# Constant multiplications on TensorE at the waits of a two-block transformer kernel on one Trainium2 core

## The reference

```python
def reference(x, ...):
    for layer in range(2):                     # first block
        h = rms_norm(x, norm1_g)
        mq, mk, mv, mo, mi, mf, aq, ak, av = split(h @ w_in)
        y_m = gated, normed mLSTM of silu(conv(mq, mk)), mv, mo, both directions
        y_a = dilated_attention(rope(aq), rope(ak), av)          # 8 heads of 64
        x = x + concat(y_m, y_a) @ w_out
        u = relu(rms_norm(x, norm2_g) @ w_up)                    # 1024 -> 4096
        x = x + (u * u) @ w_down
    x = rms_norm(x, final_g)
    x = layer_norm(ALPHA * x + pool_mixer(x))  # second block, layer 0
    x = layer_norm(ALPHA * x + swiglu(x))                        # hidden 2816
    x = layer_norm(ALPHA * x + nsa_mixer(x))   # layer 1: 16 heads, compressed,
                                               # selected and window attention
    return layer_norm(ALPHA * x + moe_ffn(x))  # 8 experts of 3584, top 2
```

## Time and profile before

| | us |
|---|---|
| median of three runs | 2382.86 (2381.65 to 2383.4) |
| profiled execution, its own time | 2385.09 |
| span of its instructions | 2383.0 |
| TensorE busy (matmuls) | 2145.7 |
| VectorE busy | 1599.2 |
| ScalarE busy | 1322.9 |

### The profile page before, as it was taken

The page is one execution under the profiler, slowest core; times in us unless marked ns, Lnnn a source line. Parts: engine busy times, 40 slices in busy tenths (PEclk is TensorE's granted clock), DMA queues, the critical chain, the costliest instruction groups (busy, mean ns, idle before and its releaser), DMA issues.

```text
span 2383.0 us, 25823 instructions
## 1 busy us (share of the span) xinstructions
PE 2145.7 (90%) x9918; PEld 1731.7 (73%) x9918; DVE 1599.2 (67%) x1539; ACT 1322.9 (56%) x1374; POOL 22.1 (1%) x33
## 2 busy tenths in 40 slices
PE   6888999988999799897868999999999888888986
PEld 5667887766888688776657887787888676766665
DVE  3865545765555545565645554887888788888987
ACT  4554444544444344445524444676776677777876
POOL 0000000000000000000000000000000000000000
PEclk9989999988999899996988999999999999999999
DMA  6314553422654345341007655798888789898995
GB/s 236 147 45 146 177 194 125 177 80 77 235 192 177 115 179 192 142 160 40 1 18 270 206 211 180 289 366 316 350 344 346 302 347 385 329 385 329 410 368 218
DMA packets 74356, 524.53 MB, mean 220 GB/s; under 512 B 8704, under 2 KB 9152, under 8 KB 11872
## 3 DMA queue, kind: packets, MB, share of 16 engines
q1 hardware_dynamic: 71424, 511.64, 56.7%
q0 software_dynamic: 2784, 10.93, 1.3%
HBM read 521.48 MB, written 1.05 MB: 219 GB/s over the span
## 4 chain that ended last, share of the span: by engine, by line
PE 71%; DVE 15%; ACT 8%; issue 5%; DMA 0%; DVEq 0%; ACTq 0%
PE psum L517 51%; PE psum L527 9%; DVE LO L507 6%; ACT HI L499 4%; PE psum L1008 2%; DVE AR L1479 1%; PE psum L2284 1%; PE psum L1013 1%; PE psum L799 1%; PE psum L2312 1%; PE psum L862 1%; DVE XT L690 1%; ACT AR L828 1%; PE psum L675 1%; PE psum L1841 1%
## 5 line engine op out<-in xcount | busy, mean ns | idle before, releaser
L507 DVE TENSOR_TENSOR LO<-ring,HI 128x2048 fp32r<-128x2048 f32 x379 | 851.7, 2258 | 453.2 <-ACT HI L499 451.1
L499 ACT ACTIVATE HI<-ring 128x2048 fp32r<-128x2048 f32 x379 | 712.7, 1886 | 369.0 <-PE psum L517 278.8
L517 PE MATMUL psum<-HI,XT 128*128 128x512 f32 (+1 forms) x2592 | 841.6, 400 | 64.6 <-DVE XT L690 30.2
L517 PEld LDWEIGHTS psum<-HI,XT 128*128 128x128 f32 x2592 | 502.5, 195 | 182.6 <-DVE XT L690 34.2
L517 PE MATMUL psum<-LO,XT 128*128 128x512 f32 (+1 forms) x1296 | 513.4, 396 | 0.0
L517 PEld LDWEIGHTS psum<-LO,XT 128*128 128x128 f32 x1296 | 253.2, 195 | 50.2
L527 PE MATMUL psum<-HI,XT 128*128 128x512 f32 x560 | 237.9, 425 | 56.5 <-DVE LO L507 55.7
L507 DVE TENSOR_TENSOR LO<-AR,HI 128x2048 fp32r<-128x2048 f32 x112 | 254.3, 2289 | 49.9 <-ACT HI L499 49.4
L499 ACT ACTIVATE HI<-AR 128x2048 fp32r<-128x2048 f32 x112 | 213.2, 1911 | 62.0 <-PE psum L527 38.0
L527 PE MATMUL psum<-LO,XT 128*128 128x512 f32 x560 | 227.9, 407 | 0.0
L517 PE MATMUL psum<-HI,HTH 128*128 128x512 f32 x568 | 225.1, 396 | 0.0
(11 more groups left out here) (271 smaller groups left out, 1829.7 us busy)
## 6 DMA issues: line engine op xcount, KB each, us to landing
ring<-in_experts SPq DMA_DIRECT2D x224, 1024.0 KB, 6.1
ring<-in_dense SPq DMA_DIRECT2D x149, 1024.0 KB, 4.8
AR<-in_experts SPq DMA_DIRECT2D x112, 1024.0 KB, 6.1
bcs<-in_ln_g POOLq DMA_DIRECT2D x4, 512.0 KB, 4.4
bcs<-in_ln_b POOLq DMA_DIRECT2D x4, 512.0 KB, 5.0
bcs<-in_norm_g POOLq DMA_DIRECT2D x3, 512.0 KB, 3.8
cons<-in_cons POOLq DMA_DIRECT2D x1, 1317.0 KB, 8.1
X<-in_x SPq DMA_DIRECT2D x2, 512.0 KB, 4.3
```

What stands on the lines that cost most here:

```text
L499: e.activation(HI[:, h:h + m], slot(u), ACT.Copy).then_inc(*high.up(u))
L507: e.tensor_tensor(LO[:, h:h + m], slot(u), HI[:, h:h + m].bitcast(F32), ALU.subtract).then_inc(*low.up(u))
L517: ins = e.matmul(out_ap, lhsT=a, rhs=b, start=start and n == 0, stop=stop and n == m - 1)
```

## The change

TensorE gets additional fp32 multiplications of constants by constants (`ident` by the first 512 columns of `cons`), written to a PSUM bank that nothing reads. `idle(e, n)` issues n of them; `idle_first(e, n)`, used while only the identity has landed, issues n of 128x128. The bank is the next of the rotation, through `Banks.hold`, without moving the rotation on; the bank is then marked "idle", and the next to hold it doesn't wait. `turn_rows` gets `wait` (multiplications before its transposes, none unless given) and `rest` (after them, one unless given).

```diff
     def hold(self, e, b, *use):
         before = self.use.get(b)
-        if before is not None:
+        if before is not None and before[0] != "idle":
             for s in self.emptied:
                 e.wait_ge(*s.of(*before))
+    def next(self, e, *use):
+        return self.hold(e, self.n % 4, *use)
...
+        def idle(e, n):
+            if n:
+                bank = banks.next(e, "idle")
+                e.wait_ge(s_cons, 16)
+                for _ in range(n):
+                    e.matmul(bank, lhsT=ident, rhs=cons[:, 0:512], start=True, stop=True)
+        def idle_first(e, n):
+            bank = banks.next(e, "idle")
+            e.wait_ge(s_ident, 16)
+            for _ in range(n):
+                e.matmul(bank[:, 0:P], lhsT=ident, rhs=ident, start=True, stop=True)
-        def turn_rows(e, name, t, src, ready):
+        def turn_rows(e, name, t, src, ready, wait=0, rest=1):
+            idle(e, wait)
...
                 ins.then_inc(*filled.up(name, "cols", t, k0))
+            idle(e, rest)
```

The places, in TensorE's order:

```diff
 # first block, layer l
+            if l == 0:
+                idle_first(e, 10)
-            turn_rows(e, n1, 0, lambda k: ROWS[:, 0, tile(k)], rows_at(n1, 0))
+            turn_rows(e, n1, 0, lambda k: ROWS[:, 0, tile(k)], rows_at(n1, 0), rest=l)
+            if l == 0:
+                idle_first(e, 18)
+            def second_rows():
+                turn_rows(e, n1, 1, lambda k: ROWS[:, 1, tile(k)], rows_at(n1, 1), wait=l, rest=l)
+                if l == 0:
+                    idle_first(e, 4)
...
             cols(e, ("aq", l), ...)
+            idle(e, 1)
             scores_tensor(e, l)
             cols(e, ("ak", l), ...)
             spread_sums_tensor(e, l, 1)
+            idle(e, 1)
             cols(e, ("av", l), ...)
...
+            def gather_last():
+                idle(e, 1)
+                ml_gather_tensor(e, l, 3)
+            steps = {1: lambda: ml_turn_tensor(e, l, 3), 2: gather_last, 7: lambda: idle(e, 1),
+                     9: lambda: idle(e, 1)}
...
 # y.l: rest=1 after tile 0, rest=0 after tile 1
 # n2.l: tile 0 rest=1; tile 1 wait=1, rest=1
 # pooling
+            idle(e, 5)                         # at the start of pool_tensor
 # l0: tile 0 wait=2, rest=3; tile 1 rest=1
 # l1: tile 0 rest=1; tile 1 wait=2, rest=1
+            idle(e, 1)                         # after cols kvc, before the turns of the queries
+                idle(e, 1 if kind or gp else 2)  # in blocks_tensor, before each of four banks
+            idle(e, 4 if qt else 2)            # at the start of turn_c_tensor
 # y.2: rest=3 after tile 0, rest=1 after tile 1
 # l2: tile 0 rest=1; tile 1 wait=6, rest=1
+            idle(e, 2)                         # at the start of route_tensor
+            idle(e, 3)                         # after route_tensor, before the first fetches
+            idle(e, 4)                         # after the fetches, before the first expert
```

More of the change, by code:

```diff
@@ L1291, in rows_at @@
                 return [v_done.of(name, "rows", t)]
-            turn_rows(e, n1, 0, lambda k: ROWS[:, 0, tile(k)], rows_at(n1, 0))
-            cols_by_tile(e, ("raw", l, 0), ("qk", l, 0), BOTH, xr, between=lambda: turn_rows(
-                e, n1, 1, lambda k: ROWS[:, 1, tile(k)], rows_at(n1, 1)))
+            if l == 0:
[7 more added lines that the diff above has]
+                    idle_first(e, 4)
+            cols_by_tile(e, ("raw", l, 0), ("qk", l, 0), BOTH, xr, between=second_rows)
             cols(e, ("raw", l, 1), ("qk", l, 1), BOTH, xr)
@@ L1313, in hybrid_tensor @@
             keys_tensor(e, l)
-            attention_tensor(e, dilated(l), {1: lambda: ml_turn_tensor(e, l, 3),
-                                             2: lambda: ml_gather_tensor(e, l, 3)})
+            def gather_last():
[3 more added lines that the diff above has]
+                     9: lambda: idle(e, 1)}
+            attention_tensor(e, dilated(l), steps)
             def y_tile(t):
                 turn_rows(e, yn, t, lambda k: Y[:, t, tile(k)],
-                          [v_bank.of(("att", l), "y", 0, t, 0), v_done.of("scaled", l)])
+                          [v_bank.of(("att", l), "y", 0, t, 0), v_done.of("scaled", l)], rest=1 - t)
             y_tile(0)
@@ L1324, in hybrid_tensor @@
                        tile1=lambda: turn_rows(e, n2, 1, lambda k: ROWS[:, 1, tile(k)],
-                                               rows_at(n2, 1)))
+                                               rows_at(n2, 1), wait=1))
         def evict(e, use, t, dst, n=512, f=ACT.Copy):
@@ L1726, in pool_tensor @@
                     ins.then_inc(*filled.up("mixed", t, nh))
-            turn_rows(e, "l0", 0, lambda k: X[:, 0, tile(k)], [v_done.of("l0", "rows", 0)])
+            turn_rows(e, "l0", 0, lambda k: X[:, 0, tile(k)], [v_done.of("l0", "rows", 0)], wait=2,
+                      rest=3)
             net_tensor(e, "ff2", "ff2", FF2_CHUNKS, BOTH, True, BA, x_ready("l0"),
@@ L1894, in sparse_tensor @@
             cols_by_tile(e, ("q0", 2), ("q0", 2), BOTH, xr, between=lambda: turn_rows(
-                e, "l1", 1, lambda k: X[:, 1, tile(k)], [v_done.of("l1", "rows", 1)]))
+                e, "l1", 1, lambda k: X[:, 1, tile(k)], [v_done.of("l1", "rows", 1)], wait=2))
             cols(e, ("q1", 2), ("q1", 2), BOTH, xr)
             cols(e, ("kvc", 2), ("kvc", 2), BOTH, xr)
+            idle(e, 1)
             for t in range(2):
@@ L1925, in y_tile @@
             def y_tile(t):
-                turn_rows(e, "y.2", t, lambda k: NY[:, t, tile(k)], [v_done.of("ny", t, 1)])
+                turn_rows(e, "y.2", t, lambda k: NY[:, t, tile(k)], [v_done.of("ny", t, 1)],
+                          rest=1 if t else 3)
             y_tile(0)
@@ L2342, in experts_tensor @@
             turn_rows(e, "l2", 0, lambda k: X[:, 0, tile(k)], [v_done.of("l2", "rows", 0)])
-            turn_rows(e, "l2", 1, lambda k: X[:, 1, tile(k)], [v_done.of("l2", "rows", 1)])
+            turn_rows(e, "l2", 1, lambda k: X[:, 1, tile(k)], [v_done.of("l2", "rows", 1)], wait=6)
             few(e, ("gates", 3), ("gates", 3), x_ready("l2"))
```

## The result

The change made the kernel slower. The changed kernel took 2396.38 us (median of 7 runs, 2390.90 to 2397.44), the kernel before, beside it on the same chip, 2386.38 (7 runs, 2381.65 to 2391.73): ratio 1.0039, 95% interval 1.0026 to 1.0052, that is 9.3 us, 6.2 to 12.4. The forecast was 5.0 us less, and its range ended at 2389.0.

The account below looks back on a forecast made before the run. TensorE carries 71% of the chain, its clock low for 179 us of the first 1280. Gains 28.8 us (30.8 less 2 for misses) minus losses 23.8 gave 5.0 us faster, 2377.8 us; range 2364 to 2389.

Parts of the forecast that it names:

- end of attention, gather at 149.07: Both layers: fillers in the waits bring back the full clock, 11.4 us gained, plus 2.0 at the gather.
- pooling, `turn_c`, y.2, l2, fetches, first expert: Fillers in waits restore the clock: gains 1.6, 1.9, 1.6, 3.5, 3.1 and 1.6 us.
- six places behind the second tile's turns: At n1.0, ff0, n1.1, ff1, ff2, q0: fillers wait for the first tile's bank, 18.9 + 3.1 us lost.
- end before VectorE's `LO`: The four fillers after the first fetches finish before VectorE's `LO`; no loss was counted.
- Where it brings a new wait: Fillers must wait for the first tile's bank to be freed, delaying second-tile products: 18.9 us at six places.
- 3.1 for the clock: Longer idling before the six products lowers the clock: 1.0 each at ff0, ff1, 1.6 at ff2, -0.5 elsewhere.
- The price of 0.9: One large added fp32 multiplication takes 0.9 us at the full clock level, 1.8 at the lower.
- The blocks' 1.4 of loss: In `blocks_tensor`, two fillers before the first turns delay ScalarE's eviction and VectorE behind it: 1.4 us lost.
- `l0`'s first tile: Three fillers wait for the bank freed by pooling's eviction: 0.4 us lost, bounds -0.5 and 1.5.
- Transposes: If transposes don't count as busy for the clock, `l1`, `y.2` and y's turning lose 7.6 us; the trace was taken to disagree.
- Rival 1: Waits for banks cost little because work behind them catches up: about 2356 us, chance 0.08.
- Rival 3: One filler in a short wait doesn't hold the clock; only mostly filled long waits gain: about 2395 us, chance 0.12.

Follow-up runs that it names:

- attention_alone: The kernel before with only the attention-end fillers, both layers (before the last mLSTM gather, steps 7 and 9, after y's first-tile turns): 2373.77 us, ratio 0.9959.
- late_alone: The kernel before with only the long-wait fillers (pooling, second `turn_c`, y.2, l2, routing, first fetches, first expert): 2372.41 us, ratio 0.9953.
- rest_alone: The kernel before with only the remaining fillers (start, norms' first turns, scores, `av`, `l0`, `l1`, queries, blocks, first `turn_c`): 2379.05 us, ratio 0.9985.
- six_alone: The kernel before with only the six fillers behind the second tile's turns, written to the first tile's bank as in the changed kernel: 2410.91 us, ratio 1.0112.
- code_before: The kernel before plus 144 never-executed instructions, placing the first expert's taken branch side where the changed kernel has it: 2389.76 us, ratio 1.0023.
- code_after: The changed kernel plus 112 never-executed instructions, placing the first expert's taken branch side where the kernel before has it: 2386.64 us, ratio 1.0010.
- own_bank: The changed kernel with the six fillers behind the second tile's turns writing to that tile's own bank, code placed as before: 2360.04 us, ratio 0.9894.
- no_between: The changed kernel without the six fillers behind the second tile's turns, code placed as before: 2359.28 us, ratio 0.9887.

## Why the prediction was wrong

The forecast's sum and what the runs give for its groups, in us (minus is faster):

| group | forecast | run | measured, 95% interval |
|---|---|---|---|
| end of attention, gather at 149.07 | -13.4 | attention_alone | -9.8 (-13.1 to -6.4) |
| pooling, `turn_c`, y.2, l2, fetches, first expert | -13.3 | late_alone | -11.2 (-14.5 to -7.6) |
| all other places | -2.3 | rest_alone | -3.6 (-6.7 to -0.5) |
| taken off for misses | +2.0 | | |
| six places behind the second tile's turns | +22.0 | six_alone | +26.7 (+23.1 to +30.5) |
| place of the code | 0 | code_before | +5.5 (+3.1 to +7.9) |
| sum | -5.0 | | +7.6 |

(-2.3 are the gains 1.5, 1.0 and 1.6 for `l1`'s first tile, less the losses 0.4 and 1.4.) Measured for the whole change: +9.3, 6.2 to 12.4. The parts add up within what they are measured to. Between the forecast and +9.3 lie 14.3 us, and no single term makes them up.

**The step that failed: that nothing costs anything but the fillers and their waits.** The prediction says that the four fillers "end before VectorE's `LO`". They did, at 1270.51 against 1272.55. What it left out is that 101 more multiplications also lengthen TensorE's code, and that the taken side of the next branch moves with it. The sum had this term at nothing. It is the largest single miss, 5.5 us by code_before (the next is 4.7, and their intervals overlap), and it is shown from both sides, by code_after and code_before. It doesn't turn the sign alone: without it the kernel is still 2.4 us slower than before (code_after), not 5.0 faster. Nothing in the trace of before said that it stood near such an edge; but it did show the two instruction loads some 6 us apart, with the DMA engines full (1.02 over 1267 to 1273 us).

**The size that was off: the clock behind the new waits.** "Where it brings a new wait" was right in mechanism, place and size: the fillers wait for the eviction, brackets of 3.22 to 6.39 us, released by ScalarE's eviction (L993, in the projections L1368) and VectorE's (L934), and the six products start 19.2 us later where 18.9 was forecast (by place 2.02 to 2.95 for the four forecast at 2.4, so the sum is nearer than its parts). The term beside it, 3.1 for the clock, measured 6.7: at `ff0`, `ff1` and `ff2` the products got longer by 2.19, 1.89 and 2.02, not by 1.0, 1.0 and 1.6, and at the other three, where -0.5 in all was forecast, they came out 0.6 longer. One filler did not keep the products fast: at `n1.1` and `ff1` it ran at the full level, and the product behind it still took 7.63. six_alone has both terms together at 26.7 where 22.0 was forecast, 23.1 to 30.5.

**The gains.** The price of 0.9 was right, and so were pooling (1.6), `l2` and the fetches. The end of attention is the interesting one: alone it gave at its place 11.5 of the 13.4 forecast, in the changed kernel only 2.7 and 2.8 in the two layers, the clock falling once more after the first gathers, and in the profiled execution of attention_alone 3.9 of the 11.5 were given back, part of it in a product that had not been slow before. The prediction took from one trace that `ff0`'s two short waits leave the clock up. In attention_alone the same two waits brought it down. And code_before, which executes the same instructions as the kernel before, shows the lower level at other places than the earlier trace rows (at 94 us, where the kernel before has none, and not at 475, where it has), with 174 us in all against 171 in the first 1260 us. So whether a short wait costs the clock differs from one execution to the next, while the sum was nearly the same in these two. Of the 3.4 us that the changed kernel lost between the traces in the experts, 1.6 are the two brackets shown above, 3.64 and 8.63. The first of them doesn't come from the code's new place, for code_after, placed as before, has 3.76 there; for the second, and for the rest, the cause stays open.

**Smaller terms.** The blocks' 1.4 of loss doesn't show: in own_bank's trace TensorE is as far ahead of the kernel before behind them (12.9 us) as in front of them (12.8). `l0`'s first tile cost 0.4 by forecast; in own_bank it took 13.66 us from the turns to the product's end and not 12.24 as before, 1.4 more, its fillers waiting for the bank until 786.94. The start and `av` were within their bounds.

**Transposes.** The prediction set the trace of before against what the Trainium skill says there (TensorE: Matmul & The Clock Gate, Part 4), that transposes don't count as busy for the clock the way matmuls do. That was too thin a ground: the stretch of the trace that spoke against it didn't stay at the full level in attention_alone. No run here separates turns from multiplications, so this stays open.

**The rivals.** Rival 1 (about 2356) falls: the waits cost all they were said to cost. Only with the waits taken away do the gains come near its number, 2360 (own_bank) and 2359 (no_between). Rival 3 had nearly the measured time, 2395, by luck: single fillers do hold the clock in attention when they stand alone (attention_alone, -9.8), though in the changed kernel they gave less than half of their 6.7 a layer. The rest of its time came about through the code and the clock behind the waits, which it doesn't name.

## What to carry to other kernels

A filler needs a destination that is already free: it waits for its bank like any other product, and everything behind it in the engine's order waits with it. Here that ate a gain of 25 to 27 us whole (code_after 1.0010 against own_bank's 0.9894); a bank that the engine holds anyway, or leaving the filler out, gave it back. The Trainium skill (TensorE: Matmul & The Clock Gate, A second HAM failure mode: psum-queue depth-cycling) tells of a kernel that loses throughput as it goes through the banks, because the engine is briefly idle between its groups and the clock falls and rises again. The brackets here are longer, 3.22 to 6.39 us, but the products behind them lost to the clock in the same way (`ff0` 7.93 us instead of 5.74).

Fill the long waits and the chains of waits, and don't count on the outcome at a short one that one trace shows as survived. And when instructions are added or taken away ahead of a branch whose taken side begins under full DMA load, look for a bracket that ends in "issue" right behind it before any other explanation of a few microseconds.

## What the runs showed of the hardware that was not expected

- Instructions that are never executed can cost 5.5 us (3.1 to 7.9): 144 of them in the untaken side moved the taken side to the end of a block of 256, and TensorE stood still until the next block had come through DMA engines that were full of weights (loads some 6 us apart, a bracket of 4.76 us in code_before and 5.72 in the changed kernel).
- Two programs with the same executed instructions (the kernel before and code_before) had some of their stretches at the lower clock at different places.
- A lower share of time at 1.2 GHz is no gain by itself: some 129 us instead of 179, and 9.3 us slower.
